# State-space groups: one break for all turned tiles, products within a chunk for two heads at a time, and another order of work where each layer enters them

## What is computed

```python
xbc = silu(causal_depthwise_conv(xbc, conv_w, conv_b))     # 4 taps
dt  = softplus(dt_raw + dt_bias);  a = -exp(a_log)
a_cum  = cumsum(dt * a)                                    # in chunks of 128 tokens
decay  = where(causal, exp(a_cum[l] - a_cum[s]), 0)
y_diag = einsum('bgrcls,bclgrp', (C @ B^T) * decay, x_dt)  # within a chunk
states = einsum('bcsgn,bgrcs,bcsgrp', B, exp(a_end - a_cum), x_dt)
prev   = scan over the 4 chunks of (h * exp(a_end) + states)
y_off  = C @ prev * exp(a_cum)                             # across chunks
y = rms_norm((y_diag + y_off + d_skip * x) * silu(z))      # by group
```

## Time and profile before

| | us |
|---|---|
| median of 3 runs (3477.98 to 3482.49) | 3481.02 |
| the profiled execution's own time | 3486.62 |
| its span in the trace | 3484.8 |
| TensorE busy | 3380.9 (97% of the span) |
| GpSimd busy | 2106.5 (60%) |
| VectorE busy | 1573.8 (45%) |
| ScalarE busy | 841.7 (24%) |

### The profile page before, as it was taken

The page is one execution under the profiler, slowest core; times in us unless marked ns, Lnnn a source line. Parts: engine busy times, 40 slices in busy tenths (PEclk is TensorE's granted clock), DMA queues, the critical chain, the costliest instruction groups (busy, mean ns, idle before and its releaser), DMA issues.

```text
span 3484.8 us, 49097 instructions
## 1 busy us (share of the span) xinstructions
PE 3380.9 (97%) x17054; PEld 2746.7 (79%) x17054; DVE 1573.8 (45%) x2898; ACT 841.7 (24%) x1723; POOL 2106.5 (60%) x2084
## 2 busy tenths in 40 slices
PE   8999999999999999998999999999999999999998
PEld 6778788887777788887888778787878887788876
DVE  6544541106544541107664652333466646423325
ACT  2223211002223211003222540322122235313321
POOL 7745577767745577765556547444855575564455
PEclk9999999999999999999999999999999999999999
DMA  3212122222211122222122222111212122121111
GB/s 134 85 61 72 62 96 96 97 97 84 85 61 72 68 93 96 99 97 90 61 84 74 84 73 92 66 67 67 97 63 85 60 97 85 61 97 61 70 64 73
DMA packets 40029, 281.41 MB, mean 81 GB/s; under 512 B 4832, under 2 KB 5344, under 8 KB 6464
## 3 DMA queue, kind: packets, MB, share of 16 engines
q1 hardware_dynamic: 38880, 277.96, 22.0%
q10 hardware_dynamic: 992, 1.31, 0.1%
HBM read 277.16 MB, written 2.10 MB: 80 GB/s over the span
## 4 chain that ended last, share of the span: by engine, by line
PE 86%; DVE 7%; issue 3%; ACT 2%; POOL 1%; DMA 0%; DVEq 0%; ACTq 0%; SPq 0%; POOLq 0%
PE banks L381 21%; PE banks L383 20%; PE banks L382 20%; PE banks L631 2%; PE banks L632 2%; PE banks L630 2%; PE banks L424 2%; PE banks L425 2%; PE banks L426 2%; PE banks L915 1%; PE banks L939 1%; PE banks L926 1%; PE banks L601 1%; PE banks L918 1%; PE banks L743 1%
## 5 line engine op out<-in xcount | busy, mean ns | idle before, releaser
L344 POOL TENSOR_SCALAR whi<-raw 128x512 fp32r<-128x512 f32 x1040 | 717.6, 699 | 1344.7 <-PE banks L383 1118.1
L349 POOL TENSOR_TENSOR wlo<-raw,whi 128x512 fp32r<-128x512 f32 x1040 | 1432.1, 1387 | 0.0
L381 PE MATMUL banks<-xhi,whi 128*128 128x512 f32 x2832 | 1145.8, 405 | 30.0 <-POOL wlo L349 19.9
L383 PE MATMUL banks<-xhi,wlo 128*128 128x512 f32 x2832 | 1109.7, 392 | 0.0
L382 PE MATMUL banks<-xlo,whi 128*128 128x512 f32 x2832 | 1108.9, 392 | 0.0
L381 PEld LDWEIGHTS banks<-xhi,whi 128*128 128x128 f32 x2832 | 535.2, 189 | 160.5 <-issue 47.0
L383 PEld LDWEIGHTS banks<-xhi,wlo 128*128 128x128 f32 x2832 | 534.4, 189 | 114.4
L382 PEld LDWEIGHTS banks<-xlo,whi 128*128 128x128 f32 x2832 | 535.7, 189 | 111.3 <-issue 8.1
L381 PE MATMUL banks<-yhi,whi 128*128 128x512 f32 x544 | 216.6, 398 | 11.2 <-DVE ylo L1675 5.6
L382 PE MATMUL banks<-ylo,whi 128*128 128x512 f32 x544 | 213.9, 393 | 0.0
L383 PE MATMUL banks<-yhi,wlo 128*128 128x512 f32 x544 | 213.8, 393 | 0.0
(11 more groups left out here) (279 smaller groups left out, 4209.4 us busy)
## 6 DMA issues: line engine op xcount, KB each, us to landing
raw<-weights SPq DMA_DIRECT2D x260, 1024.0 KB, 4.8
x<-x_in SPq DMA_DIRECT2D x4, 512.0 KB, 7.9
out<-merged SPq DMA_DIRECT2D x1, 2048.0 KB, 6.3
rot<-const SPq DMA_DIRECT2D x1, 512.0 KB, 11.5
rot<-const ACTq DMA_DIRECT2D x1, 512.0 KB, 3.6
wide_mask<-const ACTq DMA_DIRECT2D x1, 384.0 KB, 5.4
wide_mask<-const SPq DMA_DIRECT2D x1, 256.0 KB, 11.9
cst<-const SPq DMA_DIRECT2D x1, 232.0 KB, 9.2
```

Source lines behind the costliest of these rows:

```text
L344: pool.tensor_scalar(whi[p][:, w], raw[p][:, w], 1.0, 1.0, ALU.mult, ALU.mult).then_inc(s("hi_written"), 1)
L349: return pool.tensor_tensor(wlo[p][:, w], raw[p][:, w], whi[p][:, w].bitcast(F32), ALU.subtract)
L381: pe.matmul(dst, whi[p][:, w], hi[:, k, :], start=start and i == 0, stop=False)
L383: mm = pe.matmul(dst, wlo[p][:, w], hi[:, k, :], start=False, stop=stop and last_k)
```

## The change

**TensorE, turning.** In every group the three turned tiles and C times B now stand in one piece, after all eight steps of bank 3; before, three and five steps lay between them. Four steps instead of two follow.

**TensorE, within a chunk.** `within(t)` now takes two heads at once, their products alternating between the two halves of bank 6, and waits for the decays of both. `rows(2)` and `rows(3)` stand ahead of it. VectorE's order follows: both decays of the first pair, then the gate z, then both segments of the second pair, then `output(0)`.

**The entrance.** `head_columns` moves behind the whole of bank 2 and three steps of bank 3, `chunk_sums` behind the other five. The halving of the convolution's parameters and the picking of the heads' columns (`layer_setup`, `pick(0)`) move ahead of the normalisation of the tiles (`early`). The logits move from VectorE to ScalarE. ScalarE computes the last tap and the bias of three of the four convolution tiles of the first group (`conv_init`). `chunk_gaps`, `sums_lo` and `chunk_ends`, and ScalarE's `end_decays`, move behind the whole convolution.

```diff
@@ TensorE, ssm(g, first)
-                    for k in range(KT):
-                        tile_product(bank(2), 1, k, xhi, xlo, [k], start=k == 0, stop=k == KT - 1)
-                        if first and k == KT // 2 - 1:
-                            head_columns()
+                    tile_product(bank(2), 1, 0, xhi, xlo, range(KT))
+                    fill = filler([(bank(3), 1, KT), (bank(0), 0, 0), (bank(1), 0, KT)])
+                    fill(3)
+                    if first:
+                        head_columns()
+                    fill(5).then_inc(wave_done, 1)
                     if first:
                         chunk_sums()
-                    fill = filler([(bank(3), 1, KT), (bank(0), 0, 0), (bank(1), 0, KT)])
                     for t in range(3):
-                        if t:
-                            mm = fill((3, 5)[t - 1])
-                        if t == 2:
-                            mm.then_inc(wave_done, 1)
                         pe.wait_ge(s("conv"), 4 * it + t + 1)
...
-                    fill(2)
+                    fill(4)
...
-                    def within(r):
-                        if r == 0:
+                    def within(t):
+                        if t == 0:
                             pe.wait_ge(s("hstate"), it + 1)
-                        if r == 2:
+                        else:
                             pe.wait_ge(s("y_read"), 2 * it + 1)
-                        pe.wait_ge(s("decayed"), 4 * it + r + 1)
-                        o = 64 * (r % 2)
+                        pe.wait_ge(s("decayed"), 4 * it + 2 * t + 2)
                         for c in range(QB):
-                            mm = pe.matmul(psum[o:o + 64, 6, c * P:(c + 1) * P], xdt[:, c, r * 64:(r + 1) * 64],
-                                           dm[:, r % 2, c * P:(c + 1) * P], start=True, stop=True)
+                            for h in range(2):
+                                r = 2 * t + h
+                                mm = pe.matmul(psum[64 * h:64 * h + 64, 6, c * P:(c + 1) * P], xdt[:, c, r * 64:(r + 1) * 64],
+                                               dm[:, h, c * P:(c + 1) * P], start=True, stop=True)
                         mm.then_inc(s("y_within"), 1)
...
                     rows(0)
                     rows(1)
+                    fill(5)
+                    rows(2)
+                    rows(3)
+                    within(0)
+                    across(0)
                     fill(6)
-                    within(0)
-                    rows(2)
-                    fill(3)
                     within(1)
-                    across(0)
-                    rows(3)
-                    fill(4)
-                    within(2)
-                    within(3)
                     across(1)
                     fill(1).then_inc(wave_done, 1)
@@ ScalarE
+                def conv_init(g, t):
+                    tile = 2 * g + t if t < 2 else g + (8 if t == 2 else 12)
+                    if t == 0:
+                        act.wait_ge(s("ssm_ready"), L * GROUPS + 1)
+                        apart(act)
+                    if t == 2:
+                        act.wait_ge(drained[0], base + W_SSM + 5)
+                    act.activation(conv_bank(t), cbuf[:, t, 3:], ACT.Identity, scale=par[:, R_CW + 4 * tile + 3:R_CW + 4 * tile + 4],
+                                   bias=par[:, R_CB + tile:R_CB + tile + 1]).then_inc(s("conv_init"), 1)
...
-                    act.wait_ge(s("head_logits"), L + 1)
+                    own(act.activation(rates, rates, ACT.Identity, scale=par[0:48, R_SIGN:R_SIGN + 1],
+                                       bias=par[0:48, R_HB:R_HB + 1]))
+                    own.done()
                     own(act.activation(log_part, rates, ACT.Abs))
...
+                    conv_init(0, 0)
                     own(act.activation(log_part, log_part, ACT.Ln, bias=1.0))
...
                         conv_in(1, 0)
+                        conv_init(0, 2)
+                        conv_init(0, 3)
                         sums_hi()
-                        end_decays()
...
                     conv_tanh(3)
+                    if first:
+                        end_decays()
...
+                    if first:
+                        act.wait_ge(s("end_gaps"), 2 * L + 2)
+                        apart(act)
                     act.activation(cbs[:, :], bank(4), ACT.Copy).then_inc(s("ssm_evac"), 1)
@@ VectorE
-                raw_norm(L + 2 * DEPTH, {0: first_heads})
-                layer_setup()
-                head_logits()
+                def early():
+                    layer_setup()
+                    pick(0)
+                    own.done()
+
+                raw_norm(L + 2 * DEPTH, {0: first_heads}, early)
                 dve.wait_ge(wave_done, base + 2)
                 dve.tensor_tensor(cbuf[:, 0:2, 3:], bank(2, 2), spread[:, None, :].to_broadcast([P, 2, S]), ALU.mult)\
                    .then_inc(drained[1], 2)
+                dve.wait_ge(drained[1], base + W_SSM + 3)
+                dve.nop().then_inc(s("ssm_ready"), 1)
...
-                        for t in taps:
+                        for t in taps[1:2 - first // 2] if first_group else taps:
...
-                        conv_pair(2, lambda step: head_columns() if step == 1 else None)
-                        chunk_gaps()
-                        sums_lo()
-                        chunk_ends()
+                        conv_pair(2, lambda step: head_columns() if step == 2 else None)
...
                     silu(2)
                     silu(3)
+                    if first:
+                        chunk_gaps()
+                        sums_lo()
+                        chunk_ends()
...
                         if r >= 2:
-                            dve.wait_ge(s("y_within"), 4 * it + r - 1)
+                            dve.wait_ge(s("y_within"), 2 * it + 1)
...
                     segments(0)
                     segments(1)
                     decay(0)
-                    segments(2)
                     decay(1)
...
+                    segments(2)
+                    segments(3)
                     output(0)
-                    segments(3)
                     decay(2)
                     decay(3)
                     output(1)
```

More of the change, by code:

```diff
@@ L1154, in end_decays @@
                     act.wait_ge(s("chunk_sums"), L + 1)
-                    act.wait_ge(s("end_gaps"), L + 1)
+                    act.wait_ge(s("end_gaps"), 2 * L + 1)
                     own(act.activation(ends[:, 0, :, :], ends[:, 0, :, :], ACT.Exp))
@@ L1782, in first_heads @@
                     dve.nop().then_inc(drained[0], 2)
-                def head_logits():
-                    own(dve.tensor_scalar(rates, rates, par[0:48, R_HB:R_HB + 1], par[0:48, R_SIGN:R_SIGN + 1], ALU.add, ALU.mult))
-                    own.done()
-                    dve.nop().then_inc(s("head_logits"), 1)
                 def head_sums():
@@ L1810, in layer_setup @@
                     own(dve.memset(lamc[0:48, 1:2], 8.0))
+                    own(dve.tensor_scalar(par[0:48, R_HB:R_HB + 1], par[0:48, R_HB:R_HB + 1], par[0:48, R_SIGN:R_SIGN + 1], None,
+                                          ALU.mult))
                     own.done()
-                raw_norm(L + 2 * DEPTH, {0: first_heads})
-                layer_setup()
-                head_logits()
-                dve.wait_ge(wave_done, base + 2)
-                dve.tensor_tensor(cbuf[:, 0:2, 3:], bank(2, 2), spread[:, None, :].to_broadcast([P, 2, S]), ALU.mult)\
-                   .then_inc(drained[1], 2)
                 def sums_lo():
@@ L1825, in sums_lo @@
                     own.done()
+                    dve.nop().then_inc(s("end_gaps"), 1)
                 def chunk_gaps():
@@ L1843, in pick @@
                     own(dve.tensor_copy(selp[:, :].rearrange("p (h n) -> p h n", h=4), picked.to_broadcast([P, 4, 64])))
+                def early():
[3 more added lines that the diff above has]
+                raw_norm(L + 2 * DEPTH, {0: first_heads}, early)
+                dve.wait_ge(wave_done, base + 2)
+                dve.tensor_tensor(cbuf[:, 0:2, 3:], bank(2, 2), spread[:, None, :].to_broadcast([P, 2, S]), ALU.mult)\
+                   .then_inc(drained[1], 2)
+                dve.wait_ge(drained[1], base + W_SSM + 3)
+                dve.nop().then_inc(s("ssm_ready"), 1)
                 def split_y(y, name, it, g):
@@ L1853, in ssm @@
                     own.begin()
-                    pick(g)
-                    own.done()
-                    dve.nop().then_inc(s("ssm_ready"), 1)
+                    if not first:
+                        pick(g)
+                        own.done()
+                        dve.nop().then_inc(s("ssm_ready"), 1)
+                    first_group = first
                     def conv_pair(first, between):
@@ L1863, in conv_pair @@
                         dve.wait_ge(drained[1 - first // 2], n + 3 + first)
-                        for t in taps:
```

(8 more changed lines are left out.)

## The result

The changed kernel takes 3448.7 us (median of 4 runs, 3446.6 to 3452.8) against 3480.9 (4 runs, 3478.0 to 3482.5): a ratio of 0.9903, 95% interval 0.9892 to 0.9915. The forecast was 3447.4. Run again later, beside the kernel before on one chip, it gave 3449.8 against 3478.5, 0.9916 (0.9903 to 0.9930). The total is right, but two of its terms are not: the groups brought more than forecast, the entrance less. That the two errors cancel is luck.

What follows compares the result with a forecast made beforehand. TensorE, holding 86% of the chain that ended last, was taken to bound the kernel. Gains of 17.5 + 13.7 + 1.7 + 0.7 = 33.6 us took the median from 3481.0 to 3447.4 us, range 3440 to 3462.

Steps and rivals of the forecast that it cites:

- Products within a chunk: Inner products of each group: alternating two heads between array halves saves 1.71 us a group, 13.7 in 8 groups.
- Breaks: Switches between kinds of TensorE work: 24 fewer in all, taken at 0.07 us each, 1.7 us gained.
- Waits of a group: TensorE waiting for decays: the old 1.7 us goes, a new 0.1 us wait in each of 8 groups comes; net 0.7 won.
- Entrance: Start of each layer: waits at L661 and the slow clock behind them go, 18.4 us less charges, 17.5 gained.
- what is late next: Entrance after L661: VectorE ready for the states at 1635.0, TensorE there at 1635.1; 0.3 us charged per layer.
- some 2.1 us that were hidden before the silus: VectorE in the entrance: gaps, low parts of sums and chunk ends, now behind the silus, take some 2.1 us.
- the slower rival: Second pair's wait for both decays: GpSimd's splits halve VectorE's pace, 39 us more waiting plus 13 clock, 3499; chance 0.03.
- The early block: Parameters and picking before the normalisation: first layer's normalisation 0.3 to 2.4 us later, likely 0.6; 0.3 charged for both layers.
- Clock: Entrance: the lower clock behind the L661 waits, costing 1.6 us in the first layer and 2.5 in the second, goes.
- the entrance gives part back: Entrance: worst early start, later silus and states, clock down again; 10 us less gain, 3457.5; chance 0.17.
- VectorE's chain: Groups: VectorE's serial segments, output and decays bound a group; 1 us more there costs 8 us, 3455.5; chance 0.10.
- side by side: Inner products: alternating the array halves brings nothing, 13.7 us less gain, 3461.1; chance 0.05.

Runs made afterwards that it cites:

- the entrance alone: Changed entrance with the old kernel's groups (products one head at a time, steps between turned tiles), against the kernel before: 3468.2 us, ratio 0.9961.
- alternate last two: Kernel before with one edit: products of each group's third and fourth heads alternate, nothing moved: 3478.0 us, ratio 1.0004 to the kernel before.
- the picking first: Changed kernel, but heads' columns are picked before the parameters and the `keep` transfer has its own semaphore: 3451.5 us, 0.9929 to the kernel before.
- the version with the sums between the taps: Changed kernel with heads' columns picked ahead of the parameters and the sums' low parts between second and third tap pairs: 3446.8 us, 0.9911 to before.
- The version with the late signal: Changed kernel, but in each layer's first group TensorE signals `wave_done` behind the states, so GpSimd splits later: 3446.7 us, 0.9902 to the kernel before.

## Why the forecast was right, term by term

*Products within a chunk, 13.7 forecast.* Right. A group saves 3.75 - 2.05 = 1.70 in its pieces, 13.6 in eight. Of that, alternating is 1.0 a group and joining the heads 0.7. The mechanism is the one forecast, halves of the columns side by side.

*Breaks, 1.7.* Mis-sized and in the wrong place. A group saves 2.44; without 1.70 and the old wait of 0.29, some 0.45 is left, 3.6 us in eight. The two breaks of the turning hold 0.03 of it. So some 0.4 belongs to the one break fewer around the inner products and the decay rows. No run takes that part alone, but the starts in a group of before and of after place most of it: 39 products of weights among the inner pieces take 9.44 us without the wait, and now 9.16 (7.79 for the 33 left there, 1.36 for the six moved), 0.29 less; the decay rows take 2.86 and 2.80. The one break that the forecast priced like the two others is worth several of them. Why, no run shows.

*Waits of a group, net 0.7.* The old waits went, but the new one of 0.1 in each group did not come: VectorE's chain ended 4.67 us after the first piece of eight and not 5.1, and TensorE came after 4.99, forecast 5.0. From its first segment to its last decay the chain took 4.45 us, forecast 4.8: behind `output(0)` 0.15 us pass until the decays, where 0.34 passed until the segment, and the two decays take 1.29 instead of 1.47. I had kept both of these and added two semaphores. That is 1 us.

*Entrance, 17.5.* Mis-sized: 10.1 in the profiled execution, 12.9 in the second one, 13.0 with the entrance alone (1.4 of it clock elsewhere). The step that failed is "what is late next". TensorE's side was right: at the states at 37.5 us behind L449 by forecast, and at 37.7 in the second layer. VectorE was ready at 39.5, forecast 37.4. In the second layer the first product came on time (15.2, forecast 15.1), the scan 0.6 late, and then "some 2.1 us that were hidden before the silus" took 4.2. They were moved to where GpSimd works, and I gave them the duration of a row in which it had stood still for 14 us. I had the evidence, the cast of the earlier trace rows at 0.42 to 1.54, and used it for the slower rival alone. Cost: 3.7 us of wait at the states in the second run, 2.4 in the profiled execution (where the first layer waits at L661 instead), where 0.6 was charged for all.

*The early block.* The transfer landed after 4.5 us (forecast 4.2), the halving of the parameters took 1.38 (forecast 0.59, second run 0.48), the casts 2.0 (range 0.7 to 2.9), so the first layer's start was 2.5 us late, the upper end of my 0.3 to 2.4; in the second run 1.3 us. Of it 2.5 and 0.9 us are waited at L661.

*Clock.* I took the 4.1 us for granted where waits become short. In the profiled execution 1.5 us went behind the 2.5 us wait of the first layer (L661 to L666 takes 5.68 us, against 4.14 in the second), and 1.6 behind the 1.95 us of the second (group 2 at 96.86, against 95.23 in the second run).

So groups brought 3.4 more than 16.1, the entrance 4.6 to 7.4 less than 17.5, and the forecast of the total is right by offset. That the profiled executions differ by 33.8, forecast 33.6, is luck too: 4.1 of it lie in code that is not touched. The profiled execution of after lies 4.1 above its median, as before's lay 5.6 above its own. Of the rivals, "the entrance gives part back" is the one that happened, at half to three quarters of its 10 us, and the groups hid it. VectorE's chain does not bound a group, and side by side does bring something.

## What to carry to other kernels

Work that moves on one engine must be priced beside what its new neighbours on other engines do then, and not by the row of its old place; first ask which engine a faster step will set off. A piece that needs several inputs at once pays only when the last of them is early, so the order of the supplying engine is part of the edit. A forecast that is right in total can be wrong in its terms, and only halves run apart show it.

## What the runs showed of the chip

**VectorE beside GpSimd.** Operations with two operands in SBUF were lengthened when GpSimd split weights: 0.23 to 1.10 us for 64 columns, 1.39 to 2.42 for the two sums, 1.29 to 3.13 for two decays. Those with one operand in PSUM were not (0.22, and 0.68 for L1934). The halving of the parameters, which has one operand and no PSUM, was: 0.48 us in the second run, and here 1.38, until GpSimd's own operation ended (VectorE, then GpSimd):

```profile
1594.22 1.38 DVE L1817 TENSOR_SCALAR par<-par 128x104 f32<-128x104 f32 x1 [1.84 <-DMA hst<-const]
```

```profile
1594.23 1.29 POOL L349 TENSOR_TENSOR wlo<-raw,whi 128x512 fp32r<-128x512 f32 x1
```

The 64 columns lose 0.87 us, about the length of one of GpSimd's operations (0.6 to 1.3), as if they waited for one to end. The Trainium skill, SBUF — State Buffer, "SBUF: two separate sides", says so: a VectorE operation with two SBUF inputs and a GpSimd one that reads SBUF hold a shared pair of ports by turns, each for a whole instruction. The rows with two inputs agree. The section says the same of VectorE's operations in a two-port mode; whether the halving runs in one, no row shows.

**The same wait, with and without the clock.** In the sliding window of the first layer every version but one waits 1.8 to 2.1 us for VectorE (alternate last two: 1.4). TensorE's row and the clock behind it, with the picking first:

```profile
2020.33 1.11 PE L836 MATMUL banks<-cst,work 128*128 128x128 f32 x4 [1.81 <-DVEq L2067]
```

```profile
2020.33:2021.33 1.00, 1.00 (x4) 0.71 (x4) 0.00 (x0) 0.00 (x0) 1.00 (x2) 0.50 0.00 0
2021.33:2022.33 1.00, 1.00 (x11) 0.96 (x12) 0.00 (x0) 0.85 (x2) 1.00 (x2) 0.50 0.00 0
```

And in the changed kernel's second run:

```profile
2024.97 0.66 PE L836 MATMUL banks<-cst,work 128*128 128x128 f32 x4 [1.81 <-DVEq L2067]
```

```profile
2024.97:2025.97 1.00, 0.99 (x12) 0.83 (x14) 0.00 (x0) 0.30 (x1) 1.00 (x2) 1.00 0.00 0
2025.97:2026.97 1.00, 1.00 (x18) 0.75 (x13) 0.00 (x0) 0.78 (x2) 1.00 (x2) 1.00 0.06 16
```

Equal waits, and one is followed by the lower level (1.2 GHz) for 3.4 us, the other by none of it. Of the eleven profiles with such a wait in this place of the first layer, eight have the lower level behind it; of the eleven in the second layer, ten. From the end of the wait to the end of the first layer the eight take 496.5 to 497.0 us and the three others 495.1 to 495.6. None of the six waits of 1.4 us there is followed by it. The version with the sums between the taps was 1.5 us ahead at this place and lost just that here, 0.2 in a longer wait and the rest to the clock, which is why its layer has the same length (923.7 and 923.6). The version with the late signal is the only one without a fall in either layer; in the second that is 1.6 of the 2.3 us by which its layer is shorter than the second run's. What decides between the two outcomes no run shows: the operations at this place are the same. A fall costs 1.4 to 1.7 us each time, and gains of that size can't be read from the total; the place in the trace shows them.
